# Down projection with the weights' high and low parts side by side in one 512-column product

## The chip, the core and the metric

The kernel runs on one core of one Trainium2 chip. The metric is the device time of one execution in microseconds (us).

## What is computed

One layer of a hybrid encoder over 256 tokens of width 2048, in float32: a combined input projection, sliding-window attention and forgetting attention, an output projection with a residual, a gated feed-forward block of width 5632 with a residual, and a final RMSNorm. The part that the change touches is the last product and its residual:

```python
def conv_gated_ffn(h, w_up, conv_w, conv_b, w_down):
    ...
    return (jax.nn.silu(gate) * val) @ w_down
...
        x = x + conv_gated_ffn(h, w_up[l], conv_w[l], conv_b[l], w_down[l])
    return rms_norm(x, norm_final)
```

Here `gate` and `val` are each 256 x 5632, and `w_down` is 5632 x 2048.

## The kernel before

**The arithmetic.** Every weight and every activation is split into two float32r numbers: `hi`, the rounded value, and `lo`, what is left of it. A product is then three products: hi with hi, hi with lo, and lo with hi. ScalarE makes `hi` (`split_hi`, line 405), VectorE makes `lo` (`split_lo`, line 682), each for a tile of 1024 values per partition, into a ring of four slots of the tile `split`, whose first half is hi and whose second half is lo. SyncE loads the raw tiles into a ring of four slots `raw` (`load`, line 305); a load waits until the `lo` of the tile four places before is done, and `split_hi` waits until TensorE has finished the tile four places before.

**The stages in order.** Input projection and attention (to about 243 us), output projection (to about 340 us), up projection with convolution and gate (340 to 829.6 us), down projection (829.6 to 1075 us), the last norm and the stores.

**Two forms of the three products.** In `mm3` the high part of one operand is the stationary one for two matmuls, and the low part for a third; all three have 512 moving columns and write one bank of PSUM. In `features`, `tokens` and the up projection's `up_step` there are two matmuls: one with 512 moving columns, 256 of a high part and 256 of the low part of the same values, and one with 256 moving columns for the other low part. The first writes two halves of a bank, the second adds to the first half, and the two halves are added later. Both forms stream the same number of columns for the same work.

**The down projection.** The output has four groups of 512 columns (`n` = 0 to 3). A group takes 22 tiles of weights (`kt`); a tile holds two blocks of 128 rows (`c`). For each block and each of the two halves of the tokens (`m`), `down` (line 1313) calls `mm3` with `g_hi` or `g_lo` (the gated activations) as the stationary operand and the weights as the moving one. One such call for one `c` and one `m` is called a unit below: 4 units are a tile, 88 are a group. Groups 0 and 2 write the banks `sc_ps`, groups 1 and 3 the banks `tr_ps`; the first tile of a group waits by `z_s` until the group before the last one has left its banks.

**The end of a group.** VectorE waits for the group's last tile and adds the two banks to the residual `nat` (`make_z`, line 958, two additions of 512 columns). ScalarE then squares the result (`squares`, line 647), and only behind these squares stands its next `split_hi`. Five tiles later VectorE multiplies the finished columns by the norm's gain (`gain`). The last four tiles of group 3 are done first for one half of the tokens, then for the other, each followed by its own addition, norm and store.

**Semaphores.** `mm_done`, `hi_done` and `lo_done` count tiles; `z_s` counts finished halves of groups; `dve_step`, behind `st.done` and `st.wait`, orders VectorE's own results.

## Time and profile before

| | |
|---|---|
| median of 3 runs | 1083.75 us |
| the runs | 1083.64 to 1084.29 us |
| the profiled execution | 1084.46 us |
| its span, first to last instruction | 1082.7 us |
| TensorE matmul busy | 1073.4 us, 99% of the span, 6005 instructions |
| TensorE weight load busy | 919.1 us, 85% |
| VectorE busy | 722.0 us, 67% |
| ScalarE busy | 587.8 us, 54% |
| DMA, mean | 186 GB/s |

The profiled execution took 1.76 us more than its span. A matmul's recorded duration is its latency: the next one starts before it ends, so what a matmul costs is read from the distance between two starts. Weight loads run beside the matmuls. The line number of a matmul tells which of the forms it is: 1035 to 1037 are the three of `mm3`, 1047 and 1049 the pair of `features`, 1062 and 1064 the pair of `tokens`, 1295 and 1297 the pair of the up projection.

### The profile page before, as it was taken

Reading aid. Unit: us, or ns where it says so; the run is one execution under the profiler, and the core shown is the slowest. Engines: PE = TensorE matmul, PEld = TensorE weight load, DVE = VectorE, ACT = ScalarE, POOL = GpSimd, SP = SyncE. Lnnn points to the kernel's source line nnn. Section 1 sums busy time; section 2 is a strip of 40 time slices with the busy share of each in tenths; the row PEclk is TensorE's granted clock in tenths of the full one; section 3 lists DMA queues with packets and bytes.
Section 4 is the critical chain, followed back from the end, with each engine's and each line's share of the span. In section 5 each row is a group of like instructions: output and inputs, shape, how many; then the busy total and the mean of one; then the engine's idle time right before and its main releaser. Section 6 shows DMA issues by size and latency. Waiting matters only on the chain.

```text
span 1082.7 us, 17621 instructions
## 1 busy us (share of the span) xinstructions
PE 1073.4 (99%) x6005; PEld 919.1 (85%) x6005; DVE 722.0 (67%) x1058; ACT 587.8 (54%) x909; POOL 9.5 (1%) x30
## 2 busy tenths in 40 slices
PE   9999999999999999999999999999999999999997
PEld 8888888888888888888888888888888888888885
DVE  5677677676555777778777777778777444454543
ACT  6956575755555655555556555555556444343432
POOL 1000000000000000000000000000000000000000
PEclk9999999999999999999999999999999999999999
DMA  9575555554555566556655666556666655555562
GB/s 290 172 231 164 176 169 175 155 174 156 176 175 180 186 190 198 178 178 205 191 183 173 205 188 199 183 175 203 190 188 213 212 188 185 192 190 183 192 192 100
DMA packets 171329, 201.64 MB, mean 186 GB/s; under 512 B 8580, under 2 KB 138340, under 8 KB 171168
## 3 DMA queue, kind: packets, MB, share of 16 engines
q1 hardware_dynamic: 170576, 199.59, 58.8%
q0 software_dynamic: 400, 1.27, 0.5%
q8 instruction: 21, 0.34, 0.1%
q10 hardware_dynamic: 320, 0.34, 0.1%
q14 instruction: 12, 0.10, 0.0%
HBM read 199.06 MB, written 2.11 MB: 186 GB/s over the span
## 4 chain that ended last, share of the span: by engine, by line
PE 99%; DMA 0%; DVE 0%; ACT 0%; SPq 0%; DVEq 0%; issue 0%
PE tr_ps L1295 15%; PE pj L1295 15%; PE pj L1047 9%; PE pj L1297 8%; PE tr_ps L1297 8%; PE sc_ps L1035 5%; PE sc_ps L1037 5%; PE sc_ps L1036 5%; PE pj L1049 5%; PE tr_ps L1037 4%; PE tr_ps L1035 4%; PE tr_ps L1036 4%; PE pj L1062 3%; PE pj L1037 2%; PE pj L1036 2%; PE pj L1035 2%
## 5 line engine op out<-in xcount | busy, mean ns | idle before, releaser
L686 DVE TENSOR_TENSOR split<-raw,split 128x1024 fp32r<-128x1024 f32 x366 | 443.3, 1223 | 267.4 <-ACT split L409 262.8
L409 ACT ACTIVATE split<-raw 128x1024 fp32r<-128x1024 f32 x360 | 376.3, 1057 | 235.8 <-PE sc_ps L1037 78.9
L1295 PE MATMUL tr_ps<-act_split,split 128*128 128x512 f32 x704 | 245.3, 391 | 0.0
L1295 PE MATMUL pj<-act_split,split 128*128 128x512 f32 x704 | 245.0, 391 | 0.0
L1297 PE MATMUL pj<-act_split,split 128*128 128x256 f32 x704 | 197.1, 280 | 0.0
L1297 PE MATMUL tr_ps<-act_split,split 128*128 128x256 f32 x704 | 197.1, 280 | 0.0
L1295 PEld LDWEIGHTS pj<-act_split,split 128*128 128x128 f32 x704 | 131.7, 187 | 28.9
L1295 PEld LDWEIGHTS tr_ps<-act_split,split 128*128 128x128 f32 x704 | 131.7, 187 | 28.8
L1047 PE MATMUL pj<-act_split,split 128*128 128x512 f32 x416 | 148.8, 401 | 0.0
L1297 PEld LDWEIGHTS tr_ps<-act_split,split 128*128 128x128 f32 x704 | 133.1, 189 | 0.1
L1297 PEld LDWEIGHTS pj<-act_split,split 128*128 128x128 f32 x704 | 133.1, 189 | 0.0
L1049 PE MATMUL pj<-act_split,split 128*128 128x256 f32 x416 | 116.6, 280 | 0.0
L1047 PEld LDWEIGHTS pj<-act_split,split 128*128 128x128 f32 x416 | 78.2, 188 | 18.8 <-issue 0.5
L1049 PEld LDWEIGHTS pj<-act_split,split 128*128 128x128 f32 x416 | 78.6, 189 | 0.0
L1037 PE MATMUL sc_ps<-split,g_lo 128*128 128x512 f32 x176 | 69.5, 395 | 0.0
L1036 PE MATMUL tr_ps<-split,g_hi 128*128 128x512 f32 x176 | 69.5, 395 | 0.0
L1035 PE MATMUL tr_ps<-split,g_hi 128*128 128x512 f32 x176 | 69.4, 395 | 0.0
L1036 PE MATMUL sc_ps<-split,g_hi 128*128 128x512 f32 x176 | 69.4, 395 | 0.0
L1035 PE MATMUL sc_ps<-split,g_hi 128*128 128x512 f32 x176 | 69.4, 395 | 0.0
L1037 PE MATMUL tr_ps<-split,g_lo 128*128 128x512 f32 x176 | 69.4, 395 | 0.0
L630 ACT ACTIVATE conv_o<-ub,cst 128x256 f32<-128x256 f32 x88 | 48.3, 596 | 22.2 <-DVE ub L926 22.2
L640 ACT ACTIVATE g_hi<-silu 128x256 f32 (+1 forms) x44 | 16.6, 418 | 54.7 <-DVE silu L943 54.7
(200 smaller groups left out, 1187.8 us busy)
## 6 DMA issues: line engine op xcount, KB each, us to landing
raw<-w_up SPq DMA_DIRECT2D x176, 512.0 KB, 4.2
raw<-w_down SPq DMA_DIRECT2D x88, 512.0 KB, 4.5
raw<-w_in SPq DMA_DIRECT2D x72, 512.0 KB, 3.9
raw<-w_o SPq DMA_DIRECT2D x32, 512.0 KB, 4.3
nat<-x SPq DMA_DIRECT2D x8, 256.0 KB, 6.0
key_bias<-nft_dram SPq DMA_DIRECT2D x4, 512.0 KB, 5.1
result<-nat SPq DMA_DIRECT2D x7, 256.0 KB, 3.0
gfin<-norm_final POOLq DMA_DIRECT2D x1, 1024.0 KB, 7.7
```

What stands on the lines that cost most here:

```text
L409: act.activation(hi[:, slot, 0:TILE], raw[:, slot, 0:TILE], ACT.Copy).then_inc(hi_done, 1)
L630: act.activation(conv_o[:, v, b], ub[:, v, b, 2:S + 2], ACT.Identity, scale=tap(2, i * 2 + (b + v * FB)), bias=tap(3, i * 2 + (b + v * FB) ...
L640: act.activation(g_hi[:, bass.ds(i * 2 + b, 1), :].rearrange("p a n -> p (a n)"), silu[:, b], ACT.Copy).then_inc(ghi_s, 1)
L686: dve.tensor_tensor(lo[:, slot, 0:n], raw[:, slot, 0:n], hi[:, slot, 0:n].bitcast(F32), ALU.subtract).then_inc(lo_done, 1)
L1035: pe.matmul(dst, a_hi, b_hi, start=start, stop=False, skip_group_check=True)
L1036: pe.matmul(dst, a_hi, b_lo, start=False, stop=False, skip_group_check=True)
L1037: return pe.matmul(dst, a_lo, b_hi, start=False, stop=True, skip_group_check=True)
L1047: pe.matmul(bank.rearrange("p (a n) -> p a n", a=2), wh[:, c, b * P:(b + 1) * P], act_split[:, :, k, :], start=first and c == 0, stop=Fals ...
L1049: ins = pe.matmul(bank[:, 0:S], wl[:, c, b * P:(b + 1) * P], act_hi[:, k], start=False, stop=True, skip_group_check=True)
L1062: pe.matmul(bank.rearrange("p (a n) -> p a n", a=2), act_hi[:, k, rows], both[:, :, c], start=first and c == 0, stop=False, skip_group_che ...
L1295: pe.matmul(up_banks[v][b].rearrange("p (a n) -> p a n", a=2), wh[:, c, b * P:(b + 1) * P], act_split[:, :, k, :], start=k == 0, stop=Fals ...
L1297: ins = pe.matmul(up_banks[v][b][:, 0:S], wl[:, c, b * P:(b + 1) * P], act_hi[:, k], start=False, stop=True, skip_group_check=True)
```

## The change

In groups 0 to 2 of the down projection (the first three of four) the unit is no longer `mm3`. The 512 columns of the group are cut in two halves `h` of 256. For each half there is one matmul with `g_hi` as the stationary operand and 512 moving columns, the high and the low parts of the 256 weights, and one with `g_lo` and 256 moving columns, the high parts. So a unit has four matmuls and four weight loads in place of three and three, and each of the four combinations of `m` and `h` has its own bank: `sc_ps` and `pj[:, 2]`, `pj[:, 3]` for groups 0 and 2, `tr_ps` and `pj[:, 0]`, `pj[:, 1]` for group 1. At a group's end VectorE adds first the four left halves and then the four right halves to the residual (`join_z`, 8 additions of 256 columns). Group 3 keeps `mm3` and its banks `tr_ps`.

```diff
--- before.py
+++ after.py
@@ -213,6 +213,7 @@
         fox_banks = [(tr_ps[:, 0], tr_ps[:, 1]), (pj[:, 0], pj[:, 1])]
 
         up_banks = [[tr_ps[:, 0], tr_ps[:, 1]], [pj[:, 0], pj[:, 1]]]
+        down_banks = [[(sc_ps[:, 0], sc_ps[:, 1]), (pj[:, 2], pj[:, 3])], [(tr_ps[:, 0], tr_ps[:, 1]), (pj[:, 0], pj[:, 1])]]
 
 
         d_w = [sem(f"d_w{i}") for i in range(RING)]
@@ -955,12 +956,23 @@
             with dve.Fori(1, UP_STEPS) as i:
                 up_step(i, False)
 
-            def make_z(n, tiles):
-
-                bank = sc_ps if n % 2 == 0 else tr_ps
-                for m in tiles:
-                    dve.tensor_tensor(nat[:, m, n * 512:(n + 1) * 512], bank[:, m],
-                                      nat[:, m, n * 512:(n + 1) * 512], ALU.add).then_inc(z_s, 1)
+            def make_z(m):
+
+                dve.tensor_tensor(nat[:, m, 3 * 512:D], tr_ps[:, m], nat[:, m, 3 * 512:D], ALU.add).then_inc(z_s, 1)
+
+            def join_z(n):
+
+                for part in range(2):
+                    if part == 1:
+                        st.wait()
+                    for m in range(MT):
+                        for h in range(2):
+                            cols = nat[:, m, n * 512 + h * 256:n * 512 + (h + 1) * 256]
+                            ins = dve.tensor_tensor(cols, down_banks[n % 2][m][h][:, part * 256:(part + 1) * 256], cols, ALU.add)
+                            if part == 0:
+                                st.done(ins)
+                        if part == 1:
+                            ins.then_inc(z_s, 1)
 
             def gain(n):
 
@@ -976,7 +988,7 @@
                 n, kt = divmod(t, DOWN_TILES)
                 if kt == DOWN_TILES - 1 and n < 3:
                     dve.wait_ge(mm_done, T_DOWN + t + 1)
-                    make_z(n, range(MT))
+                    join_z(n)
                 if kt == 4 and n > 0:
                     if n == 1:
                         dve.wait_ge(d_gf, 16)
@@ -987,7 +999,7 @@
                     dve.tensor_scalar(part3, small[:, 26:28], 1.0 / D, EPS, ALU.mult, ALU.add).then_inc(part_s, 1)
             for m in range(MT):
                 dve.wait_ge(last_s, m + 1)
-                make_z(3, [m])
+                make_z(m)
                 dve.wait_ge(z_s, 2 * 3 + m + 5)
                 st.done(dve.tensor_tensor(z_gain[:, m], nat[:, m, 3 * 512:D], gfin[:, 3 * 512:D], ALU.mult))
                 dve.wait_ge(z_root, m + 1)
@@ -1310,15 +1322,28 @@
             with pe.Fori(1, UP_STEPS) as i:
                 up_step(i, False)
 
-            def down(n, kt, tiles):
-
-                bank = sc_ps if n % 2 == 0 else tr_ps
-                slot = (n * DOWN_TILES + kt) % RING
+            def down(n, kt):
+
+                both = split[:, :, (n * DOWN_TILES + kt) % RING, 0:TILE].rearrange("p a (c n) -> p a c n", c=2)
+                for c in range(2):
+                    for m in range(MT):
+                        for h in range(2):
+                            b, rows, bank = 2 * kt + c, slice(m * P, (m + 1) * P), down_banks[n % 2][m][h]
+                            cols = slice(h * 256, (h + 1) * 256)
+                            pe.matmul(bank.rearrange("p (a n) -> p a n", a=2), g_hi[:, b, rows], both[:, :, c, cols],
+                                      start=kt == 0 and c == 0, stop=False, skip_group_check=True)
+                            ins = pe.matmul(bank[:, 0:256], g_lo[:, b, rows], both[:, 0, c, cols], start=False, stop=True,
+                                            skip_group_check=True)
+                return ins
+
+            def down_last(kt, tiles):
+
+                slot = (3 * DOWN_TILES + kt) % RING
                 wh, wl = wide(hi, slot), wide(lo, slot)
                 for c in range(2):
                     for m in tiles:
                         b = 2 * kt + c
-                        ins = mm3(bank[:, m], g_hi[:, b, m * P:(m + 1) * P], g_lo[:, b, m * P:(m + 1) * P],
+                        ins = mm3(tr_ps[:, m], g_hi[:, b, m * P:(m + 1) * P], g_lo[:, b, m * P:(m + 1) * P],
                                   wh[:, c], wl[:, c], start=kt == 0 and c == 0)
                 return ins
 
@@ -1329,13 +1354,14 @@
                     if kt == 0:
                         pe.wait_ge(z_s, 2 * n + 2)
                     pe.wait_ge(lo_done, T_DOWN + n * DOWN_TILES + kt + 1)
-                    down(n, kt, range(MT)).then_inc(mm_done, 1)
+                    ins = down(n, kt) if n < 3 else down_last(kt, range(MT))
+                    ins.then_inc(mm_done, 1)
 
             for m in range(MT):
                 for kt in range(DOWN_TILES - LAST, DOWN_TILES):
                     if m == 0:
                         pe.wait_ge(lo_done, T_DOWN + 3 * DOWN_TILES + kt + 1)
-                    ins = down(3, kt, [m])
+                    ins = down_last(kt, [m])
                 ins.then_inc(last_s, 1)
```

TensorE's order where the up projection ends and the down projection begins, before (`g_hi`, `g_lo` are the gated activations, `split` the weights, the left name is the bank that is written):

```order
L1295 MATMUL pj<-act_split,split 128x512
L1297 MATMUL pj<-act_split,split 128x256
L1310 REGISTER_ALU
L1310 COMPARE_AND_BRANCH
L1035 MATMUL sc_ps<-split,g_hi 128x512
L1036 MATMUL sc_ps<-split,g_hi 128x512
L1037 MATMUL sc_ps<-split,g_lo 128x512
L1035 MATMUL sc_ps<-split,g_hi 128x512
```

and with the change:

```order
L1307 MATMUL pj<-act_split,split 128x512
L1309 MATMUL pj<-act_split,split 128x256
L1322 REGISTER_ALU
L1322 COMPARE_AND_BRANCH
L1333 MATMUL sc_ps<-split,g_hi 128x512
L1335 MATMUL sc_ps<-split,g_lo 128x256
L1333 MATMUL sc_ps<-split,g_hi 128x512
L1335 MATMUL sc_ps<-split,g_lo 128x256
L1333 MATMUL pj<-split,g_hi 128x512
L1335 MATMUL pj<-split,g_lo 128x256
```

Three matmuls of 512 columns became two of 512 and two of 256, and the bank changes after each pair of them.

VectorE's order at the end of group 0, before (the first row is the `split_lo` of the tiles of that group, the last ones are the splits of the next tiles and the gain):

```order
L686 TENSOR_TENSOR split<-raw,split 128x1024 x21
L962 TENSOR_TENSOR nat<-sc_ps,nat 128x512 x2
L686 TENSOR_TENSOR split<-raw,split 128x1024 x5
L969 TENSOR_TENSOR nat<-nat,gfin 128x512 x2
L686 TENSOR_TENSOR split<-raw,split 128x1024 x17
```

and with the change:

```order
L687 TENSOR_TENSOR split<-raw,split 128x1024 x21
L971 TENSOR_TENSOR nat<-sc_ps,nat 128x256 x2
L971 TENSOR_TENSOR nat<-pj,nat 128x256 x2
L971 TENSOR_TENSOR nat<-sc_ps,nat 128x256 x2
L971 TENSOR_TENSOR nat<-pj,nat 128x256 x2
L687 TENSOR_TENSOR split<-raw,split 128x1024 x5
L981 TENSOR_TENSOR nat<-nat,gfin 128x512 x2
```

The additions stand at the same place; two of 512 columns became eight of 256, the second four of which follow a wait for the first four. Groups 1 and 2 have the same pattern.

## Rows read from the trace of the kernel before

**Rows 1.** The page: busy time by engine, granted clock, chain that ended last.

```profile
PE 1073.4 (99%) x6005; PEld 919.1 (85%) x6005; DVE 722.0 (67%) x1058; ACT 587.8 (54%) x909; POOL 9.5 (1%) x30
...
PEclk9999999999999999999999999999999999999999
...
PE 99%; DMA 0%; DVE 0%; ACT 0%; SPq 0%; DVEq 0%; issue 0%
```

**Rows 2.** Lines 1035 and 1037 (down projection): duration ns min/median/max, first and last start us, forms.

```profile
L1035 PE MATMUL sc_ps<-split,g_hi x176: 390/393/405, 829.6 to 1013.0; 128*128 128x512 f32 x176
...
L1037 PE MATMUL tr_ps<-split,g_lo x176: 390/393/405, 891.4 to 1074.8; 128*128 128x512 f32 x176
```

**Rows 3.** Line 1295 (up projection), the same view.

```profile
L1295 PE MATMUL pj<-act_split,split x704: 390/391/392, 352.6 to 829.3; 128*128 128x512 f32 x176
```

**Rows 4.** Timeline of PE where up ends and down begins: start us, duration us.

```profile
829.27 0.39 PE L1295 MATMUL pj<-act_split,split 128*128 128x512 f32 x1
829.50 0.28 PE L1297 MATMUL pj<-act_split,split 128*128 128x256 f32 x1
829.62 0.39 PE L1035 MATMUL sc_ps<-split,g_hi 128*128 128x512 f32 x1
...
830.31 0.39 PE L1035 MATMUL sc_ps<-split,g_hi 128*128 128x512 f32 x1
```

**Rows 5.** Timeline of PE, input projection, 44.3 to 73.4 us.

```profile
44.29 0.24 PE L1226 MATMUL tr_ps<-ident,prob 88*128 88x88 f32 x1
44.32 0.48 PE L1047 MATMUL pj<-act_split,split 128*128 128x512 f32 x1
...
44.75 0.40 PE L1047 MATMUL pj<-act_split,split 128*128 128x512 f32 x1
...
72.31 0.40 PE L1047 MATMUL pj<-act_split,split 128*128 128x512 f32 x1
...
72.66 0.40 PE L1062 MATMUL pj<-split,act_split 128*128 128x512 f32 x1
...
73.02 0.40 PE L1062 MATMUL pj<-split,act_split 128*128 128x512 f32 x1
...
73.37 0.40 PE L1062 MATMUL pj<-split,act_split 128*128 128x512 f32 x1
```

**Rows 6.** Timeline of PE, input projection, 96.9 to 98.9 us.

```profile
96.86 0.40 PE L1047 MATMUL pj<-act_split,split 128*128 128x512 f32 x1
...
97.21 0.39 PE L1047 MATMUL pj<-act_split,split 128*128 128x512 f32 x1
...
98.94 0.39 PE L1047 MATMUL pj<-act_split,split 128*128 128x512 f32 x1
```

**Rows 7.** Groups of VectorE: count, busy us, mean ns, idle before.

```profile
L686 DVE TENSOR_TENSOR split<-raw,split 128x1024 fp32r<-128x1024 f32 x366 | 443.3, 1223 | 267.4 <-ACT split L409 262.8 <-ACT split L417 4.4
...
L921 DVE TENSOR_TENSOR up_r<-up_r,tr_ps 128x256 f32<-128x256 f32 x44 | 16.5, 417 | 18.3 <-ACT up_r L626 18.3
...
L962 DVE TENSOR_TENSOR nat<-sc_ps,nat 128x512 f32<-128x512 f32 x4 | 2.6, 685 | 0.8 <-PE sc_ps L1037 0.8
```

**Rows 8.** Timeline of VectorE around the end of group 0.

```profile
889.53 1.23 DVE L686 TENSOR_TENSOR split<-raw,split 128x1024 fp32r<-128x1024 f32 x1 [1.57 <-ACT split L409]
891.16 1.29 DVE L962 TENSOR_TENSOR nat<-sc_ps,nat 128x512 f32<-128x512 f32 x2 [0.40 <-PE sc_ps L1037]
894.21 2.36 DVE L686 TENSOR_TENSOR split<-raw,split 128x1024 fp32r<-128x1024 f32 x2 [1.76 <-ACT split L409]
```

**Rows 9.** Timeline of ScalarE around the same end.

```profile
891.89 0.63 ACT L652 ACTIVATE sq_out<-nat 128x512 f32<-128x512 f32 x1 [2.38 <-DVE nat L962]
...
893.13 1.99 ACT L409 ACTIVATE split<-raw 128x1024 fp32r<-128x1024 f32 x2
```

## The prediction

> **What bounds the kernel now.** I read the page first. TensorE's matmuls fill 99% of the span, the chain that ended last is 99% TensorE, and the granted clock is at its full level, 2.4 GHz, in all 40 slices [rows 1]. So no wait of another engine ends last anywhere near the change: what counts is how many columns TensorE streams and at what distance the matmuls start. A matmul's own duration (390 ns) is a latency and says nothing of that; I take the distance of starts over long stretches.
>
> In the down projection the first matmul starts at 829.6 us and the last at 1074.8 us, and there are 4 x 22 x 12 = 1056 of them, so 245.2 / 1055 = 232.4 ns each [rows 2]. A unit of three takes 697.2 ns. There is no gap among them to win: the even distance leaves none, and where up ends and down begins the starts go on without a pause (829.50, 829.62, 830.31) [rows 4].
>
> The form that the change brings in already runs in the up projection, right before. From pass 0's second half to the end there are 1376 pairs of one 512-column and one 256-column matmul, with starts at 352.6 to 829.3 us: 476.7 / 1375 = 346.7 ns per pair [rows 3]. Inside a pair the step from the 512 to the 256 is about 230 ns (829.27 to 829.50) and from the 256 to the next 512 about 117 ns (829.50 to 829.62) [rows 4].
>
> The same form also runs in the input projection, slower. From 44.75 to 72.66 us there are 79 pairs, 27.91 / 79 = 353.3 ns each, and the rate stays the same where the operands are swapped at 72.66 us, from weights stationary (line 1047) to activations stationary and weights moving (line 1062): 72.31, 72.66, 73.02, 73.37 [rows 5]. A little later line 1047 runs six pairs in 98.94 - 96.86 = 2.08 us, 346.7 ns each, as in the up projection [rows 6]. So there are two rates for one form, 346.7 and 353.3 ns, and the kind of operand does not choose between them.
>
> **The change part by part.** It concerns 3 groups x 22 tiles x 4 = 264 units.
>
> *Columns.* Before: 3 x 512 = 1536 per unit. After: 2 x (512 + 256) = 1536. Nothing is saved here. The price can move only by the distance per column.
>
> *Matmuls.* A unit becomes two pairs. At the up projection's rate that is 2 x 346.7 = 693.4 ns, 3.9 ns less than 697.2 with the unrounded rates, and 264 x 3.9 = 1.0 us less. At the slower rate it is 2 x 353.3 = 706.6 ns, 9.4 ns more, and 264 x 9.4 = 2.5 us more. These two are the ends for this term; the trace of before has nothing of this form outside them over a long stretch. By its operands (weights moving, activations stationary) the nearest row is that of line 1062, which ran at the slow rate; by what goes before it the nearest is the up projection. I choose the second: in rows 5 the slow rate had set in after something else came between, a group of transposes (line 1226) and a first matmul with a longer distance, 44.32 to 44.75 us, and from there it kept through tile borders and a change of operands. In the up projection the fast rate keeps through 1375 pairs, 21 passes of a loop and all its waits. At 829.6 us nothing comes between: the last pair of up is followed at once by a pair of down. Neither side explains what sets the rate, so this is a choice by neighbourhood, and the price of the other value is kept in the range.
>
> *Weight loads.* Four per unit in place of three, 264 more. They cost nothing as long as each lies beside a matmul. The cover is the 117 ns of a 256-column matmul, and the up projection shows that it is enough: there too every second matmul has 256 columns, each has its own weight load, and the pair takes no more than its share of columns. The other rate is the price if it is not quite enough.
>
> *The join.* Two additions of 128x512 at 685 ns become eight of 128x256. The nearest row is an addition of 256 columns with an operand in PSUM, 417 ns [rows 7]: 8 x 0.42 = 3.3 us in place of 1.3 us, so 2.0 us more on VectorE at each of three ends. Is it covered? At the end of a group the last matmul starts just before 890.9 us, VectorE adds from 891.16 [rows 8], ScalarE squares from 891.89 and makes the next high part from 893.13 us [rows 9], and the low part follows from 894.21 us [rows 8]. This tile is the fourth after the end; TensorE has three tiles before it, 3 x 4 x 0.697 = 8.4 us, so it needs the tile at 899.3 us. Before, it was ready at 895.4 us. With the change the second half of the tokens is joined at 891.16 + 3.3 = 894.5 us, its square takes until about 895.2, the high part until 896.2, the low part until 897.4 us. That leaves 1.9 us. Even at 685 ns per addition, the other bound, the join ends at 896.7 us and the tile is ready at 899.6 us, 0.3 us late, three times: 0.9 us. I take nothing for this term. What would be late next is the load that waits for this low part, and its tile is used four tiles later, 11 us on.
>
> *Banks.* The join of group n reads its four banks while TensorE writes the other four, so TensorE does not wait for it as long as the join ends within a group (61 us). Group 3 goes on in `tr_ps`, free since the end of group 1. The last group, the norm and the stores are not touched.
>
> **The sum.** Against the profiled execution's own 1084.46 us: -1.0 + 0 + 0 = 1083.4 us. That execution is 0.7 us above the median of the runs shown, 1083.75, and by that median the same sum gives 1082.7 us. A measurement of this kernel can tell from no change about 0.2%, which is 2.2 us. So the forecast is a gain too small to be told.
>
> **The rivals.**
>
> *The slow rate, slower than before.* In groups 0 to 2 the pairs run at 353.3 ns. For it: it is the rate of the only rows with this choice of operands, and the down projection before already has 232.4 ns per 512 columns where up has 230. Against it: the swap at 72.66 us changed nothing in the rate, and line 1047 has both. It gives 1083.75 + 2.5 = 1086.2 us. It decides from where the pairs stay above 352.7 ns in all three groups (2.2 us / 528 = 4.1 ns over the present 348.6 per 768 columns); in a part of the groups alone it stays under the bound.
>
> *A fixed part per matmul.* The unit has one matmul more for the same columns. In the up rows the 256-column matmul takes 117 ns and the 512-column one 230, so that 2 x 117 - 230 = 4 ns do not shrink with the columns (3 with unrounded steps). If the down projection keeps its own price per column and pays that for each added matmul, the sum is 264 x 3 = +0.8 us and the time 1084.6 us. For it: it is plain arithmetic on the rows. Against it: the pair of up has this part in it, and is still below one and a half times 232.4. The Trainium skill states the same (TensorE: Matmul & The Clock Gate, section "Wait — 56ns, not 53.3ns?"): a fixed cost of about 2.5 ns per back-to-back matmul at the full clock. By that figure alone the 264 added matmuls would cost an estimated 0.7 us, against the change; the distances in these rows are all longer than the page's formula gives (it says 215.7 ns for 512 columns, the rows show 230 to 232), so here the measurement decides.
>
> *The join holds up a split.* The additions cost 0.69 us each or more, or the squares start later than worked out. Then TensorE pauses once after each of three group ends, 0.3 us each by the bound above and up to some 2 us if the load behind it is late as well: 1084 to 1088 us.
>
> *A larger gain.* The extra 2.3 ns of each 512-column matmul in down come from writing one bank many times in a row or from something else that four banks remove, and the pairs run below 346.7 ns. No row shows this. A gain over 2.2 us would need pairs below 344.5 ns. That the change does not do what it says I leave out: the order of the instructions shows it.
>
> **How the numbers follow.** The up projection's rate 0.55 (1082.7 us); the slow rate 0.22 (1086.2 us); the fixed part 0.13 (1084.6 us); a late split 0.05 (1084 to 1088 us); a larger gain 0.05 (below 1081.6 us). Slower by over 0.2%: the slow rate lies hardly above the bound, so most of its chance and a part of the late split's, in all 0.22. Faster by over 0.2%: the larger gain and a little for the spread of the runs, 0.06. The rest, 0.72, is no change that can be told. The range takes in the forecast less 0.5 us for the spread of the runs (0.65 us) and reaches to the slow rate: 1082.2 to 1086.4 us.
>
> **What would show it.** In the trace of after: pairs of down at 346.7 ns and 88 units of a group in 61.0 us (61.4 before); group 3 still at 232.4 ns; eight additions of about 0.42 us and the fourth split after a group's end ready by 897.5 us in the same place; no distance of starts above 0.25 us at the group ends. Pairs with a repeated pattern around 353 ns would show the slow rate, and pauses of TensorE some 8 us after a group's end the late split. The prediction is wrong if the three groups together take less than 181.9 or more than 186.3 us (184.1 before).

## The result, and the profile after

The changed kernel takes 1085.56 us (median of 22 runs, 1084.47 to 1086.33), the kernel before 1083.62 us (22 runs, 1082.69 to 1084.38). The ratio is 1.0017, 95% interval 1.0011 to 1.0022: slower by 1.9 us, which is clear of the noise and still under the 0.2% that the prediction took as its bound. The profiled execution took 1084.74 us. Single executions of one kernel differ by about 2 us here, so what a part of the kernel costs is read below from the starts in the traces and not from totals.

The page of the changed kernel, the lines that answer to [rows 1]:

```profile
PE 1073.6 (99%) x6269; PEld 930.8 (86%) x6269; DVE 726.1 (67%) x1076; ACT 587.9 (54%) x909; POOL 9.5 (1%) x30
...
PEclk9999999999999999999999999999999999999999
...
PE 99%; DMA 0%; DVE 0%; ACT 0%; issue 0%; DVEq 0%; SPq 0%
```

The engines and the clock are as before; there are 264 matmuls and 264 weight loads more. TensorE is still the whole chain, so the time must lie in the distance of its starts. The lines of the up projection (1307), of the new unit's 512-column matmul (1333) and of group 3 (1047, 1049), which answer to [rows 2, 3], duration ns min/median/max and then first and last start in us:

```profile
L1307 PE MATMUL pj<-act_split,split x704: 390/391/392, 351.3 to 827.9; 128*128 128x512 f32 x176
...
L1333 PE MATMUL sc_ps<-split,g_hi x176: 387/396/398, 828.3 to 1012.6; 128*128 128x512 f32 x176
...
L1047 PE MATMUL tr_ps<-split,g_hi x88: 387/396/399, 1013.7 to 1074.6; 128*128 128x512 f32 x88
...
L1049 PE MATMUL tr_ps<-split,g_lo x88: 392/395/399, 1014.1 to 1075.0; 128*128 128x512 f32 x88
```

Up: (827.9 - 351.3) / 1375 = 346.6 ns per pair, as before. Groups 0 to 2 last from 828.3 to 1013.7 us, the first start of group 3: 185.4 us for 528 pairs, 351.1 ns each, against 184.1 us before (792 x 232.4 ns). Group 3, whose instructions did not change, takes 1075.0 - 1013.7 = 61.3 us for 263 distances, 233.3 ns each, against 232.4 before: 0.2 us more. Together the trace shows 1.3 + 0.2 = 1.5 to 1.6 us of the 1.9 between the medians. The rest is within what single executions differ by.

TensorE's timeline where up ends and down begins (start us, duration us), beside [rows 4], and 22 us later:

```profile
827.93 0.39 PE L1307 MATMUL pj<-act_split,split 128*128 128x512 f32 x1
828.16 0.28 PE L1309 MATMUL pj<-act_split,split 128*128 128x256 f32 x1
828.28 0.39 PE L1333 MATMUL sc_ps<-split,g_hi 128*128 128x512 f32 x1
828.51 0.28 PE L1335 MATMUL sc_ps<-split,g_lo 128*128 128x256 f32 x1
828.63 0.40 PE L1333 MATMUL sc_ps<-split,g_hi 128*128 128x512 f32 x1
828.87 0.28 PE L1335 MATMUL sc_ps<-split,g_lo 128*128 128x256 f32 x1
```
```profile
850.04 0.40 PE L1333 MATMUL pj<-split,g_hi 128*128 128x512 f32 x1
850.28 0.28 PE L1335 MATMUL pj<-split,g_lo 128*128 128x256 f32 x1
850.40 0.39 PE L1333 MATMUL pj<-split,g_hi 128*128 128x512 f32 x1
850.62 0.28 PE L1335 MATMUL pj<-split,g_lo 128*128 128x256 f32 x1
850.74 0.40 PE L1333 MATMUL sc_ps<-split,g_hi 128*128 128x512 f32 x1
850.98 0.28 PE L1335 MATMUL sc_ps<-split,g_lo 128*128 128x256 f32 x1
851.10 0.40 PE L1333 MATMUL sc_ps<-split,g_hi 128*128 128x512 f32 x1
```

The first pair of down still takes 0.35 us (828.28 to 828.63), but in the second pair the step behind the 512-column matmul is 0.24 us (828.63 to 828.87) where it was 0.23. Twenty microseconds later a fixed rhythm of three pairs is there: 240, 120, 220, 120, 240 and 120 ns by the rounded starts, 850.04 to 851.10. It runs on over the borders of tiles. No distance between two starts is above 0.24 us anywhere in the three groups. There is no pause to explain, only a slightly longer step.

VectorE and ScalarE at the end of group 0, which answer to [rows 8, 9]:

```profile
890.27 0.76 DVE L971 TENSOR_TENSOR nat<-sc_ps,nat 128x256 f32<-128x256 f32 x2 [0.43 <-PE pj L1335]
890.94 0.75 DVE L971 TENSOR_TENSOR nat<-pj,nat 128x256 f32<-128x256 f32 x2
891.72 0.76 DVE L971 TENSOR_TENSOR nat<-sc_ps,nat 128x256 f32<-128x256 f32 x2
892.40 0.74 DVE L971 TENSOR_TENSOR nat<-pj,nat 128x256 f32<-128x256 f32 x2
894.88 3.50 DVE L687 TENSOR_TENSOR split<-raw,split 128x1024 fp32r<-128x1024 f32 x3 [1.74 <-ACT split L410]
```
```profile
892.51 0.63 ACT L653 ACTIVATE sq_out<-nat 128x512 f32<-128x512 f32 x1 [3.93 <-DVE nat L971]
...
893.80 1.99 ACT L410 ACTIVATE split<-raw 128x1024 fp32r<-128x1024 f32 x2
```

TensorE's first matmul of the tile that these two engines make ready, the fourth of group 1:

```profile
898.50 0.40 PE L1333 MATMUL tr_ps<-split,g_hi 128*128 128x512 f32 x1
```

The eight additions take 2.9 us (890.27 to 893.14) in place of 1.3, a row of two about 0.75 us. The squares start at 892.51 against 891.89 us before, with a group end that is 0.9 us earlier in this trace, so they are 1.5 us later behind the group's end. The next high part starts at 893.80, and the low part, the first of the three that start at 894.88, is done at about 896.1 us. TensorE starts on it at 898.50 us, 2.4 us later. The join is hidden.

### The profile page after: what moved, and what is told of

It is laid out like the page before. It is cut to its first block, busy times and chain, and to the rows that moved or that the text cites. A ratio compares the mean times of both kernels' runs of the same rounds, so it can differ in the third digit from the quotient of the medians.

```text
span 1082.9 us, 18167 instructions
## 1 busy us (share of the span) xinstructions
PE 1073.6 (99%) x6269; PEld 930.8 (86%) x6269; DVE 726.1 (67%) x1076; ACT 587.9 (54%) x909; POOL 9.5 (1%) x30
## 4 chain that ended last, share of the span: by engine, by line
PE 99%; DMA 0%; DVE 0%; ACT 0%; issue 0%; DVEq 0%; SPq 0%
PE tr_ps L1307 15%; PE pj L1307 15%; PE pj L1059 9%; PE pj L1309 8%; PE tr_ps L1309 8%; PE pj L1333 6%; PE pj L1061 5%; PE sc_ps L1333 4%; PE pj L1335 3%; PE pj L1074 3%; PE sc_ps L1335 2%; PE tr_ps L1049 2%; PE tr_ps L1048 2%; PE tr_ps L1047 2%; PE tr_ps L1333 2%; PE pj L1047 2%
## 5 line engine op out<-in xcount | busy, mean ns | idle before, releaser
L410 ACT ACTIVATE split<-raw 128x1024 fp32r<-128x1024 f32 x360 | 376.2, 1057 | 232.8 <-PE pj L1335 96.9
L1333 PE MATMUL pj<-split,g_hi 128*128 128x512 f32 x264 | 98.3, 394 | 0.0
L1335 PE MATMUL pj<-split,g_lo 128*128 128x256 f32 x264 | 74.7, 283 | 0.0
L1333 PE MATMUL sc_ps<-split,g_hi 128*128 128x512 f32 x176 | 65.5, 394 | 0.0
L1333 PEld LDWEIGHTS pj<-split,g_hi 128*128 128x128 f32 x264 | 49.6, 188 | 11.5
L1335 PE MATMUL sc_ps<-split,g_lo 128*128 128x256 f32 x176 | 49.8, 283 | 0.0
L1335 PEld LDWEIGHTS pj<-split,g_lo 128*128 128x128 f32 x264 | 49.7, 188 | 0.0
```

The costliest lines, as they stand in the source:

```text
L410: act.activation(hi[:, slot, 0:TILE], raw[:, slot, 0:TILE], ACT.Copy).then_inc(hi_done, 1)
L1333: pe.matmul(bank.rearrange("p (a n) -> p a n", a=2), g_hi[:, b, rows], both[:, :, c, cols], start=kt == 0 and c == 0, stop=False, skip_gro ...
L1335: ins = pe.matmul(bank[:, 0:256], g_lo[:, b, rows], both[:, 0, c, cols], start=False, stop=True, skip_group_check=True)
```

## The experiments

The theories, as they stood before the first four of these kernels ran. **A**: the moving reads of `split` cost, because other engines write it. **B**: a rhythm that depends on what went before and then keeps. **C**: the step between the two places of the 512-column read costs. **D**: each matmul has a fixed part. All rates below are taken from starts, as above: from the first start of group 0 to the first start of group 3, by the number of pairs. Where no number of runs is given, a time is that of one execution.

### Moving operand that nobody writes

```diff
-pe.matmul(bank.rearrange("p (a n) -> p a n", a=2), g_hi[:, b, rows], both[:, :, c, cols],
+pe.matmul(bank.rearrange("p (a n) -> p a n", a=2), g_hi[:, b, rows], g_hi[:, 0:18:17, :],
...
-ins = pe.matmul(bank[:, 0:256], g_lo[:, b, rows], both[:, 0, c, cols], start=False, stop=True,
+ins = pe.matmul(bank[:, 0:256], g_lo[:, b, rows], g_hi[:, 0], start=False, stop=True,
```

> The moving operand of groups 0 to 2 is read from blocks 0 and 17 of g_hi, which nobody writes in this stage, in place of the weights in split; the result is then not the reference's. Everything else, waits and splits included, stays. Theory A, the moving reads of split cost time because ScalarE and VectorE write it meanwhile: the pair falls from 351.1 ns to the 346.7 ns of the up projection, the three groups take 183.1 us and the run about 2.3 us less than the changed kernel. Theory B, the rate depends on which form of matmuls runs with which history and not on what the others write: 351.1 ns stay.

Measured: 1086.0 us in one execution (the kernel before 1082.95 on the same chip).

```profile
L1333 PE MATMUL sc_ps<-g_hi x176: 395/398/403, 828.6 to 1014.1; 128*128 128x512 f32 x176
...
L1047 PE MATMUL tr_ps<-split,g_hi x88: 390/393/404, 1015.2 to 1075.8; 128*128 128x512 f32 x88
```

1015.2 - 828.6 = 186.6 us by these rounded starts, 186.55 us by the trace's nanoseconds, 353.3 ns per pair: slower, not faster. Theory A is out. Theory B's 351.1 ns did not come either: changing nothing but the source of the moving operand changed the rate. And group 3 behind it, with the same instructions as ever, ran at (1075.8 - 1015.2) / 87 / 3 = 232.2 ns, the rate of the kernel before.

This execution also shows something in code that no kernel of this study touches, the input projection (start us, duration us):

```profile
59.67 0.40 PE L1059 MATMUL pj<-act_split,split 128*128 128x512 f32 x1
...
60.71 0.39 PE L1059 MATMUL pj<-act_split,split 128*128 128x512 f32 x1
```

Three pairs in 1.04 us, 346.7 ns each; in the kernel before the same instructions at the same place took 353.3 ns [rows 5]. These are two programs, but one program does the same. Two executions of the kernel with the order 512, 512, 256, 256 (below), the first and then the timed one:

```profile
44.26 0.40 PE L1059 MATMUL pj<-act_split,split 128*128 128x512 f32 x1
...
58.12 0.40 PE L1059 MATMUL pj<-act_split,split 128*128 128x512 f32 x1
```
```profile
44.29 0.40 PE L1059 MATMUL pj<-act_split,split 128*128 128x512 f32 x1
...
58.42 0.40 PE L1059 MATMUL pj<-act_split,split 128*128 128x512 f32 x1
```

Forty pairs take 13.86 us in one, 346.5 ns each, and 14.13 us in the other, 353.3 ns each. So one and the same program can take either rate there.

### One run of 512 in place of two of 256

```diff
-g_hi[:, b, rows], both[:, :, c, cols],
+g_hi[:, b, rows], both[:, 0:1, c, :].rearrange('p a (x n) -> p (a x) n', x=2),
```

> The 512-column matmul reads 512 high parts in one run in place of 256 high and 256 low parts from two places; the result is not the reference's. Theory C, the step between the two places costs: the pair falls from 351.1 ns to 348.6 or less. Theories A and B: 351.1 ns stay.

Measured: 1084.82 us; groups 0 to 2 from 828.4 to 1013.8 us, 351.1 ns per pair, group 3 at 233.3 ns. In the whole down projection no distance between two starts differs from the changed kernel's by more than 2 ns. Theory C is out.

### Every matmul of 256 columns

```diff
-ins = mm3(bank[:, m], g_hi[:, b, m * P:(m + 1) * P], g_lo[:, b, m * P:(m + 1) * P],
-          wh[:, c], wl[:, c], start=kt == 0 and c == 0)
...
+for h in range(2):
+    cols = slice(h * 256, (h + 1) * 256)
+    ins = mm3(bank[:, m, cols], g_hi[:, b, m * P:(m + 1) * P], g_lo[:, b, m * P:(m + 1) * P],
+              wh[:, c, cols], wl[:, c, cols], start=kt == 0 and c == 0 and h == 0)
```

> The kernel before with each 512-column matmul of groups 0 to 2 cut in two of 256: six matmuls per unit, the same banks, columns and result. Theory D, each matmul has a fixed part of about 3 ns: the unit takes 697.2 + 3 x 3 = 706 ns and the kernel 2.4 us more than the kernel before. If the fixed part is nothing, 697 ns and no change; if short matmuls uncover the weight loads, over 720 ns and more than 6 us.

Measured: 1087.09 us (the kernel before 1082.95).

```profile
L1035 PE MATMUL sc_ps<-split,g_hi x352: 279/281/287, 828.3 to 1015.9; 128*128 128x256 f32 x176
...
L1035 PE MATMUL tr_ps<-split,g_hi x264: 279/282/404, 891.0 to 1076.9; 128*128 128x256 f32 x88, 128*128 128x512 f32 x44
```

Group 0 takes 891.0 - 828.3 = 62.7 us, 712 ns per unit against 697.2: 14.8 ns for three added matmuls, 4.9 each. The changed kernel has one more and pays 702.2 - 697.2 = 5.0 ns. Groups 0 to 2 are cut so, group 3 is not. So far Theory D, with a larger part than expected. The weight loads stay covered at 119 ns per matmul.

### Breaks in the rhythm

Four matmuls of 128 columns ahead of group 0, then in two other kernels one short matmul ahead of each tile from the fifth on, in the new form and in the old.

```diff
+def pause():
+    for _ in range(4):
+        pe.matmul(sc_ps[:, 0, 0:P], ones[:], ident[:], start=True, stop=True, skip_group_check=True)
...
+if n == 0 and kt == 0:
+    pe.wait_ge(z_s, 2)
+    pause()
```

> The changed kernel with four short matmuls of 128 columns between the up projection and group 0, their output overwritten. Theory B (what came just before sets the rate, which then keeps): the pair in groups 0 to 2 goes to another of the rates, 346.7, 350 or 353.3 ns. Theories A, C and D: 351.1 ns stay, and the only cost is some 0.3 to 0.5 us for the four matmuls.

Measured: 1086.09 us.

```profile
L1333 PE MATMUL sc_ps<-split,g_hi x176: 387/396/476, 829.6 to 1014.0; 128*128 128x512 f32 x176
...
L1047 PE MATMUL tr_ps<-split,g_hi x88: 387/396/398, 1015.0 to 1075.9; 128*128 128x512 f32 x88
```

1015.0 - 829.6 = 185.4 us: 351.1 ns, although the first matmul after the break started 0.31 us before its partner (829.58 and 829.89 us). The rate came back.

```diff
+if n < 3 and kt >= 4:
+    ...
+    spare = (tr_ps, sc_ps)[n % 2]
+    pe.matmul(spare[:, 0, 0:16 + 6 * (kt - 4)], ones[:], ones[:, 0:16 + 6 * (kt - 4)], start=True, stop=True, skip_group_check=True)
```

> The changed kernel with one short matmul (16 to 118 columns, longer by 6 at each tile) ahead of each of the tiles 4 to 21 of groups 0 to 2, written into a bank that nobody needs then. Each breaks the rhythm at another phase. Theory B: the pairs take different rates from tile to tile, among them 346.7 and 353.3 ns. If 351.1 ns is the price of the form in this stage, every tile returns to 351.1. The time goes up by the 54 breaks, which is of no interest.

> The same breaks in the kernel before, whose 512-column matmuls ran at 232.4 ns (348.5 per 768 columns). Theory B: here too the rate differs from tile to tile (348.5 and 350.0 are known); what counts is then the mean over the tiles beside that of the new form with the same breaks. A mean difference of 2.6 ns per 768 columns would say that the new form costs more whatever the phase; none would say that the 2 us were the phase alone.

Measured: 1096.94 us for the new form and 1095.83 us for the old, with 54 breaks each. In the new form all 54 tiles show nearly the same mean from the second pair behind the break to the last of the tile, 350.0 to 350.2 ns per pair, whatever the length of the break. From the fourth pair on, the distances are those of the old rhythm of three pairs again. So Theory B, as put, fails for the new form in the down projection: a break does not give another rate. For the old form it holds in part: from the second matmul behind the break its tiles vary from 347.2 to 350.1 ns per 768 columns, mean 348.9. With the same breaks the new form still costs 1.3 ns per pair more; groups 0 to 2 take 197.5 us against 196.2. The expectation had named 2.6 ns for a price of the form and none for the phase alone; this is half of it and decides for neither.

### The operands' places as in the up projection, and two banks

```diff
-pe.matmul(bank.rearrange("p (a n) -> p a n", a=2), g_hi[:, b, rows], both[:, :, c, cols],
+k = (2 * m + h) * P
+pe.matmul(bank.rearrange("p (a n) -> p a n", a=2), both[:, 0, c, k:k + P], g_hi[:, 0:18:17, :],
...
-ins = pe.matmul(bank[:, 0:256], g_lo[:, b, rows], both[:, 0, c, cols], start=False, stop=True,
+ins = pe.matmul(bank[:, 0:256], both[:, 1, c, k:k + P], g_hi[:, 0], start=False, stop=True,
```

> Groups 0 to 2 keep their pairs, waits and banks, but the operands take the places that they have in the up projection: the weights in split are stationary (128 columns at a time, high and low), blocks 0 and 17 of g_hi are moving. The result is not the reference's. Theory F, which operand is stationary sets the price of a pair: 346.7 ns, and the run about 2.3 us below the changed kernel. Theory G, the place in the program or the four banks set it: 351 ns or more stay.

Measured: 1085.62 us (the kernel before 1084.19).

```profile
L1334 PE MATMUL sc_ps<-g_hi,split x176: 387/396/398, 829.4 to 1013.8; 128*128 128x512 f32 x176
...
L1047 PE MATMUL tr_ps<-split,g_hi x88: 390/393/405, 1014.8 to 1075.5; 128*128 128x512 f32 x88
```

1014.8 - 829.4 = 185.4 us, 351.1 ns. Which of these operands is stationary does not matter. Group 3 is at 232.4 ns here, not 233.3.

```diff
-down_banks = [[(sc_ps[:, 0], sc_ps[:, 1]), (pj[:, 2], pj[:, 3])], [(tr_ps[:, 0], tr_ps[:, 1]), (pj[:, 0], pj[:, 1])]]
+down_banks = [[(sc_ps[:, 0], sc_ps[:, 0]), (sc_ps[:, 1], sc_ps[:, 1])], [(tr_ps[:, 0], tr_ps[:, 0]), (tr_ps[:, 1], tr_ps[:, 1])]]
...
-          start=kt == 0 and c == 0, stop=False, skip_group_check=True)
+          start=kt == 0 and c == 0 and h == 0, stop=False, skip_group_check=True)
```

> The changed kernel with both halves of a unit written into one bank, so that groups 0 to 2 use two banks each as the up projection does; the left and right halves are summed into each other, so the result is not the reference's. If going round four banks costs, the pair falls from 351.1 towards 346.7 ns; if banks do not matter, it stays at 351.1.

Measured: 1084.96 us, 351.1 ns per pair (828.5 to 1013.9 us), 233.3 ns in group 3. Banks do not matter in the new form. Nor do they in the old, with the bank, and with it the stationary operand, changed after every matmul of groups 0 to 2:

```diff
+for part, (left, right) in enumerate(((g_hi, wh), (g_hi, wl), (g_lo, wh))):
+    for m in tiles:
+        ins = pe.matmul(bank[:, m], left[:, b, m * P:(m + 1) * P], right[:, c],
+                        start=kt == 0 and c == 0 and part == 0, stop=part == 2, skip_group_check=True)
```

> The kernel before, its three matmuls of a unit interleaved for the two halves of the tokens, so that the bank changes after every matmul; same result. If a change of bank costs or saves, the 512-column matmul moves from 232.4 ns by over 1 ns; if not, the run is within 0.3 us of the kernel before in the down projection.

Measured: 1083.53 us (1084.19 before), groups 0 to 2 from 828.7 to 1012.7 us, 184.0 us, as in the kernel before.

### The same four matmuls in another order

```diff
-        for h in range(2):
-            b, rows, bank = 2 * kt + c, slice(m * P, (m + 1) * P), down_banks[n % 2][m][h]
-            cols = slice(h * 256, (h + 1) * 256)
-            pe.matmul(bank.rearrange("p (a n) -> p a n", a=2), g_hi[:, b, rows], both[:, :, c, cols],
-                      start=kt == 0 and c == 0, stop=False, skip_group_check=True)
-            ins = pe.matmul(bank[:, 0:256], g_lo[:, b, rows], both[:, 0, c, cols], start=False, stop=True,
-                            skip_group_check=True)
+        b, rows, banks = 2 * kt + c, slice(m * P, (m + 1) * P), down_banks[n % 2][m]
+        for h in range(2):
+            pe.matmul(banks[h].rearrange("p (a n) -> p a n", a=2), g_hi[:, b, rows], both[:, :, c, h * 256:(h + 1) * 256],
+                      start=kt == 0 and c == 0, stop=False, skip_group_check=True)
+        for h in range(2):
+            ins = pe.matmul(banks[h][:, 0:256], g_lo[:, b, rows], both[:, 0, c, h * 256:(h + 1) * 256], start=False, stop=True,
+                            skip_group_check=True)
```

> The same four matmuls per unit in the order 512, 512, 256, 256; the result is the same. If the prices add up by size, as the unit of six 256s (712.0 ns) and of three 512s (697.2 ns) say, 2 x 232.4 + 2 x 118.7 = 702.2 ns, the same as in the changed kernel, which also took 702.2. If what counts is a 256 behind a 512 and its weight load, or the two writes of one bank in a row, another value by more than 2 ns.

> The order 512, 512, 256, 256 again, timed. Its one look showed 348.3 ns per 768 columns in groups 0 to 2, 0.2 less than the kernel before, and 348.5 in group 3: 0.1 us less than the kernel before in the down projection, no difference that can be measured, and 1.7 us less than the changed kernel. If the rate is drawn anew in each run, the profile of this run shows another one than 348.3.

Measured: 1083.18 us in the first run; timed, 1083.71 us (11 runs) against 1083.68 of the kernel before (15 runs), ratio 1.0000, interval 0.9991 to 1.0009. The profile of the timed kernel:

```profile
L1332 PE MATMUL sc_ps<-split,g_hi x176: 392/392/393, 828.4 to 1011.2; 128*128 128x512 f32 x176
...
L1047 PE MATMUL tr_ps<-split,g_hi x88: 390/393/404, 1012.4 to 1073.0; 128*128 128x512 f32 x88
```

1012.4 - 828.4 = 184.0 us for groups 0 to 2, where the kernel before took 184.1 and the changed kernel 185.4; group 3 at 232.2 ns. The same four matmuls and weight loads, the same banks and the same join, in another order, cost nothing. This ends Theory D as well: there is no price of an added matmul that holds in every order, for one was added per unit and none was paid. It also settles that the join is hidden, since it is the same here. What is not told apart: the new order puts the two sizes in another sequence, and it has the same stationary operand for two matmuls in a row. Both executions show 348.3 ns per 768 columns, so the rate was not another one in the second.

### The new form in group 0 alone

```diff
-ins = down(n, kt) if n < 3 else down_last(kt, range(MT))
+ins = down(n, kt) if n < 1 else down_last(kt, range(MT), n)
```

(`down_last` and the addition at a group's end take the group's bank, as before the change.)

> The new form in group 0 alone; groups 1 to 3 are as in the kernel before. In the changed kernel group 3, whose instructions are the same as before, ran at 350.0 ns per 768 columns in place of 348.5. Theory B, the rate is a rhythm that is handed on until something breaks it: groups 1 to 3 all run at 350.0. If it was something of group 3 itself (its banks, its wait), groups 1 and 2 run at 348.5.

Measured: 1083.58 us. Group 0 takes 61.8 us (828.3 to 890.1), groups 1 to 3 run at 232.4 ns. So Theory B's 350.0 ns did not come: the longer step of group 3 in the changed kernel is not handed on by every end of a new group. But it is not something of group 3 itself either, the expectation's other case, for group 3 is at 232.4 ns here too. The run with breaks in the up projection (next section) shows more: its instructions from group 0 on are those of the changed kernel, and group 3 took 232.4 ns there, not 233.3. So group 3's rate is set either by what ran before the down projection, which had changed, or anew from execution to execution.

### Is it the stage, the pattern of addresses, or the loop?

Groups 0 to 2 with all that the up projection's instructions have:

```diff
+wh, wl = narrow(hi, slot), narrow(lo, slot)
+for c in range(4):
+    for b in range(2):
+        k, bank = (4 * kt + c) % 16, (sc_ps, tr_ps)[n % 2][:, b]
+        pe.matmul(bank.rearrange("p (a n) -> p a n", a=2), wh[:, c, b * P:(b + 1) * P], g_hi[:, k:k + 17:16, :],
+                  start=kt == 0 and c == 0, stop=False, skip_group_check=True)
+        ins = pe.matmul(bank[:, 0:256], wl[:, c, b * P:(b + 1) * P], g_hi[:, k], start=False, stop=True,
+                        skip_group_check=True)
```

> Groups 0 to 2 copy the up projection's instructions in all that it has: eight pairs per tile, weights in split stationary in four blocks of rows, moving blocks k and k+16 of g_hi (256 columns each, at the distance that the halves of act_split have), two banks in turn. The result is not the reference's. Theory H, a pattern of addresses and banks sets the rate, and the looks that copied parts of it missed one: 346.7 ns. Theory I, the stage sets it, whatever the form's details: 351 ns or more, as in the look with the roles of up.

Measured: 1085.72 us (1083.71 before).

```profile
L1333 PE MATMUL sc_ps<-g_hi,split x352: 387/396/400, 829.5 to 1014.6; 128*128 128x512 f32 x176
...
L1047 PE MATMUL tr_ps<-split,g_hi x88: 390/393/404, 1014.9 to 1075.5; 128*128 128x512 f32 x88
```

1014.9 - 829.5 = 185.4 us, 351.1 ns: operands' roles, blocks, distances and turn of banks are copied, only the tensor that is moving and which banks are written differ, and still it is the rate of the down projection.

Short matmuls as breaks in the up projection's loop:

```diff
+if not first and s % 2 == 1:
+    pe.matmul(pj[:, 2, 0:16 + 12 * s], ones[:], ones[:, 0:16 + 12 * s], start=True, stop=True, skip_group_check=True)
```

> The changed kernel with a short matmul (28 to 100 columns) in tiles 1, 3, 5 and 7 of each pass of the up projection's loop, into a bank that is free there. If 346.7 ns belongs to the form in this stage, the pairs return to 346.7 after each break, as the pairs of the down projection returned to their own rhythm. If it is one of several rhythms and the loop had fallen into a good one, the pairs take 350 to 353 ns after some or all breaks.

Measured: 1108.67 us, with 84 breaks. TensorE's timeline over two of them (start us, duration us):

```profile
601.90 0.30 PE L1313 MATMUL pj<-ones 128*128 128x28 f32 x2
...
602.47 0.40 PE L1307 MATMUL tr_ps<-act_split,split 128*128 128x512 f32 x1
...
607.32 0.40 PE L1307 MATMUL tr_ps<-act_split,split 128*128 128x512 f32 x1
...
607.67 0.32 PE L1313 MATMUL pj<-ones 128*128 128x52 f32 x2
...
608.24 0.40 PE L1307 MATMUL pj<-act_split,split 128*128 128x512 f32 x1
...
611.77 0.40 PE L1307 MATMUL pj<-act_split,split 128*128 128x512 f32 x1
```

Fourteen pairs from 602.47 to 607.32 us are 346.4 ns each; after the next break ten pairs from 608.24 to 611.77 us are 353 ns each. The two alternate from break to break through all passes of the loop: behind each break of 28 or 76 columns the pairs take 346.6 or 346.7 ns, behind each of 52 or 100 columns 352.7 or 352.8, taken over the whole stretch but its first pair. So in the up projection Theory B does hold: 346.7 ns is not the price of the form but one of at least two rhythms, and the loop had fallen into the good one.

The loop itself: the down projection's groups 0 and 1 as a loop of 11 passes on TensorE, and the up projection written out.

```diff
+with pe.Fori(0, 11) as i:
+    for s in range(4):
+        pe.wait_ge(lo_done, i * 4 + (T_DOWN + s + 1))
+        ...
```

> The changed kernel with groups 0 and 1 of the down projection as a loop on TensorE, 11 passes of 4 tiles, in place of 44 tiles written out. All passes use the first eight blocks of g and the banks of group 0, so the result is not the reference's; pairs, ring and waits are those of the changed kernel. Theory J, code written out one time is what makes the pair 351.1 ns, and a loop body that is run again is cheaper: about 346.7 ns over most of the 123 us. Otherwise 351.1 ns stay, as in group 2, which is written out here too.

```diff
-with pe.Fori(1, UP_STEPS) as i:
+for i in range(1, UP_STEPS):
     up_step(i, False)
```

> The changed kernel with the up projection's loop written out on TensorE alone (21 passes of 64 pairs, the same matmuls). Theory J: the up projection's pair goes from 346.7 to about 351.1 ns, and the run becomes 21 x 64 x 4.4 ns = 5.9 us longer. If the loop does not matter, 346.7 ns stay and nothing changes.

Measured: 1085.75 and 1085.47 us (the kernel before 1084.25). In the first, groups 0 to 2 take 1014.7 - 829.3 = 185.4 us. In the second the up projection stays at (828.7 - 352.0) / 1375 = 346.7 ns:

```profile
L1307 PE MATMUL pj<-act_split,split x704: 391/391/391, 352.0 to 828.7; 128*128 128x512 f32 x176
```

The loop does not matter.

### The operands moved by 128 bytes

One thing sorted all runs so far with the order 512, 256: the tensor pairs. `split` with `act_split` ran at 346.7 or 353.3 ns and `g_hi` with itself at 353.3; `split` with `g_hi` and `g_lo` settled at 351.1, in either role. What differs is where the tensors begin.

```diff
+sb("gap", [P, 32])
 region = sbuf.cursor
```

> The changed kernel with 128 unused bytes per partition ahead of g_hi. Before, split and act_split start at a multiple of 1024 bytes and g_hi and g_lo at 896 past one (105344 and 150400 bytes above the start); with the gap all four start at a multiple. Theory K, the place of the stationary operand against the moving one, counted within 1024 bytes, sets which rhythms a pair can take: pairs of split with act_split and of g_hi with itself (0 apart) ran at 346.7, 347 and 353.3 ns, all pairs of split with g_hi or g_lo (896 apart) at 351.1, in either role. It expects that 351.1 ns is gone from groups 0 to 2: either 346.7 ns, 2.3 us less than the changed kernel, or 353.3 ns, 1.2 us more. If 351.1 ns stay, the place has nothing to do with it and the cause is open.

> The kernel before with the same gap. Theory K: the 512-column matmuls leave 232.4 ns (348.5 per 768 columns) too, in either direction by a few ns per 768 columns; if they stay, the matmuls of one size do not depend on the place, or Theory K is wrong.

Measured: the changed kernel with the gap 1090.59 us (5 runs), ratio to the kernel before 1.0066, interval 1.0052 to 1.0079. The kernel before with the gap 1084.0 us (11 runs) against 1083.79 (15 runs), ratio 1.0001, interval 0.9992 to 1.0010. The changed kernel with the gap:

```profile
L1308 PE MATMUL pj<-act_split,split x704: 395/398/403, 348.1 to 833.9; 128*128 128x512 f32 x176
...
L1334 PE MATMUL sc_ps<-split,g_hi x176: 395/398/403, 834.3 to 1019.8; 128*128 128x512 f32 x176
...
L1048 PE MATMUL tr_ps<-split,g_hi x88: 389/389/395, 1020.8 to 1080.0; 128*128 128x512 f32 x88
```

Groups 0 to 2: 1020.8 - 834.3 = 186.5 us by the rounded starts, 186.56 by the trace's nanoseconds, 353.3 ns per pair. The 351.1 ns are gone, as Theory K said, and it is the worse of its two values. Group 3, the old form: (1080.0 - 1020.8) / 87 / 3 = 226.8 ns where it was 233.3. The whole kernel became 5.0 us slower than the changed kernel, not 1.2, for the up projection changed as well. The kernel before with the gap:

```profile
L1296 PE MATMUL pj<-act_split,split x704: 395/398/403, 348.3 to 834.1; 128*128 128x512 f32 x176
...
L1036 PE MATMUL sc_ps<-split,g_hi x176: 389/389/395, 834.5 to 1013.3; 128*128 128x512 f32 x176
...
L1036 PE MATMUL tr_ps<-split,g_hi x176: 389/389/389, 894.3 to 1073.2; 128*128 128x512 f32 x176
...
L1038 PE MATMUL tr_ps<-split,g_lo x176: 388/389/389, 894.8 to 1073.6; 128*128 128x512 f32 x176
```

A group takes 894.3 - 834.5 = 59.8 us in place of 61.3, and the four groups 1073.6 - 834.5 = 239.1 us in place of 245.2, which is 239.1 / 1055 = 226.7 ns per matmul. So 128 bytes are worth some 6 us in the down projection of the kernel before. They are lost again in the up projection, (834.1 - 348.3) / 1375 = 353.3 ns per pair in place of 346.7, 9.1 us, although neither of its two operands moved; only what runs before it (the output projection reads `mix_hi`, which moved too) and the other engines' tensors did. That is the other rhythm which the breaks had shown. The output projection gives 2.0 us back (94.4 us between its first and last start in place of 96.4), and what lies before it the rest, since the whole comes out even.

Two limits of this. In the changed kernel with the gap, the up projection too ran at 353.3 ns, with the same six distances in turn, right up to the first pair of down. So for the pair a rhythm handed over from the up projection is a rival that these runs do not exclude. For the 512-column matmul they do: behind groups at 353.3 ns group 3 took 232.2 ns without the gap (the run with the moving operand that nobody writes) and 226.8 with it. And the distance within 1024 bytes, as Theory K counts it, does not fit: the slots of `split` lie 4352 bytes apart, 256 past a multiple of 1024, so that distance changes with every tile, while the rhythm of three pairs runs on over the tiles. What stays the same over the slots is the distance within 256 bytes, 128 without the gap and 0 with it.

## Why the prediction was wrong

**What held.** TensorE alone sets the time; there was no pause to win. Columns are equal. The weight loads are covered beside 256-column matmuls, at 119 ns in the run with six of them per unit. The join is hidden, and cheaper than worked out: 2.9 us, not 3.3, and the fourth split is ready 2.4 us before its use, not 1.9. Group ends show no distance above 0.25 us. The time, 1085.56 us, lies in the range.

**What failed.** The step is the one in "Matmuls": "I choose the second", the rate of the up projection because "nothing comes between". The forecast was a gain of 1.0 us, the runs show a loss of 1.9. The pair went to 351.1 ns instead of 346.7, and the change begins in the second pair of the stage. 528 x (351.1 - 348.6) = 1.3 us in place of -1.0, and 0.2 us more in group 3, for which I had nothing. The rate is not carried over from the stage before: a break makes it return to 351.1, and a copy of the up projection's form takes it too. The loss against the kernel before belongs to the order 512, 256, 512, 256: with the same operands at the same places the order 512, 512, 256, 256 took 184.0 us for the three groups, as before the change, and lost nothing. The start of the operands counts too: with `g_hi` and `g_lo` 128 bytes further on, the pair no longer took 351.1 ns. Neither of the two readings of the rows gave the rate, not what goes before and not the operands' roles.

**The ends.** I wrote that nothing of this form lay outside 346.7 and 353.3 ns, and 351.1 lies within; taking the two as the only values for the sum and the first rival was the second mistake.

**The rivals.** The slow rate (353.3 ns, 1086.2 us) had the right sign, place and kind, but its term was 2.5 us where groups 0 to 2 lost 1.3, and its total lay 0.6 us above the measured one; it did come, in the kernel with the gap and in the one with `g_hi` moving. The fixed part (1084.6 us) seemed to be confirmed twice, with 4.9 and 5.0 ns per added matmul in place of 3, and the order 512, 512, 256, 256 then showed that no such part holds in every order: one matmul added, nothing paid. For the same reason the Trainium skill's 2.5 ns per back-to-back matmul (TensorE: Matmul & The Clock Gate, section "Wait — 56ns, not 53.3ns?") does not describe these streams: the same 1536 columns took 680 ns in three matmuls with the gap, 697.2 without it, and in four matmuls 702.2 or 696.7 by the order alone.

**What stays open.** Shown is that the place of `g_hi` and `g_lo` changes the rate of the 512-column matmul in the down projection, and that in up and in the input projection one stream can take two rates. That the place changes the pair's rate as well is likely and not shown. Why 128 bytes or an order of four matmuls do this is not shown; other gaps were not tried. What makes the up projection enter one rhythm or the other is open too, and why group 3 took 233.3 ns behind some new groups and 232.4 behind others. A version with the gap and the up projection kept in its good rhythm was not tried; if both hold together, the kernel before with the gap would take an estimated 9.1 us less than its 1084.0, from the 9.1 us above.

## What to carry to other kernels

When TensorE is 99% busy, compare the distance of starts between stages that do the same work: 226.7 to 233.3 ns for one and the same matmul over the runs here is 3% that no view of waits shows. Before a form is swapped for its rate in another stage, see whether that form has several rates in the trace; if so, the rate belongs to the place and not to the form, and only a run decides. Two cheap things to vary are the order of the matmuls in a unit and the start of an operand's tensor. Here the order took back the loss of 1.9 us, and the start moved 6 us from one stage to another; neither made the kernel faster than it was before.

## What was not expected of the hardware

- With `g_hi` and `g_lo` 128 bytes further on, a 512-column float32r matmul took 226.7 ns in place of 232.4, and the pair of 512 and 256 took 353.3 ns in place of 351.1, behind an up projection that had changed as well.
- The same pair of matmuls has steady rhythms of 346.7 and 353.3 ns that last for hundreds of pairs. In the up projection a short matmul between switches them (84 breaks, in turn); in the down projection, with other tensors, 54 breaks left the pair's 351.1 ns as they were.
- The untouched input projection ran from 44 to 77 us at 353.3 ns in some executions and at 346.7 in others, also in two executions of one and the same program.
- A fourth matmul for the same 1536 columns cost 5.0 ns in the order 512, 256, 512, 256 and nothing in the order 512, 512, 256, 256.
